# Adding the weights onto their negated high part by a transfer, in ten chunks of a down projection

## The chip, the cores and the metric

The kernel runs on one core of one Trainium2 chip. The metric is the device time of one execution in microseconds (us). The engines of the core work side by side and wait for one another by semaphores: TensorE multiplies matrices, VectorE and ScalarE work element by element, GpSimd does the same and issues transfers from a queue of its own, and SyncE issues the other transfers.

## The reference

Two layers on 512 tokens of width 1024, all in float32. Layer 0 is latent attention and then a gated feed-forward block; layer 1 is a short convolution and then another such block. What matters here is the end of the feed-forward block of layer 0, the product with `w_down`:

```python
def swiglu(h, w_gate, w_up, w_down):
    return (jax.nn.silu(h @ w_gate) * (h @ w_up)) @ w_down

for i in range(DEPTH):
    ...
    h = h + swiglu(rms_norm(h, ffn_norm[i]), ffn_w_gate[i], ffn_w_up[i], ffn_w_down[i])
return rms_norm(h, final_norm)
```

`w_down` has 2816 rows (D_FF, 22 blocks of 128) and 1024 columns.

## The kernel before

**Products in three parts.** Every float32 operand is split into a high part, rounded to the format fp32r, and the rest, operand minus high part. A product is three matmuls, high by high, low by high and high by low (`product`, lines 489 to 491), summed in a PSUM bank.

**Chunks and slots.** The weights lie in memory as one stream of chunks of up to 2048 columns on 128 partitions (1 MB). Chunks go alternately to two slots, s = 0 and 1. Each slot has `raw[s]`, where the transfer lands, and `w_hi[s]` and `w_lo[s]`, the high part and the rest, both inside a buffer that the profile calls split. A chunk j of a stage lives in slot j % 2 and passes these steps:

- SyncE's `load` (issue at line 363) waits for `w_split[s]` of the chunk before in the same slot, since until then raw is still read, and fetches the next chunk.
- ScalarE's `split` (line 937) waits until raw has landed and until TensorE is done with the chunk before in the same slot (`chunk_done[s]`), copies raw to `w_hi[s]` and raises `hi_split[s]`.
- The rest, raw minus `w_hi[s]`, goes to `w_lo[s]` and raises `w_split[s]`. In this stage VectorE makes it (line 1445). In the attention stage GpSimd does (line 460).
- TensorE waits once per chunk for `w_split[s]`, multiplies, and raises `chunk_done[s]`.

**The down projection of layer 0** takes 12 chunks, here called chunks 0 to 11. Four pairs of output tiles take three chunks each: 8, 8 and 6 blocks of rows, so 2048, 2048 and 1536 columns. A chunk of 2048 columns is 48 matmuls of 512 columns, one of 1536 is 36. Chunks 2, 5, 8 and 11 are the short ones. The two slots mean that chunk j is split while chunk j - 1 is multiplied. So chunks 3, 6 and 9, which are long, are split during a short one.

**What sets the order.** Each engine has one fixed order, and nothing is scheduled at run time. ScalarE runs `residuals`, which splits chunk c + 2 in its step c, with sizes `DOWN_AHEAD` = 1536, 2048, 2048, repeated, and squares the finished sums in every third step. In steps 9 to 11 it also prepares operands of the convolution (`conv_operands`). VectorE runs `down_round`: in every third step it adds two finished tiles to the residual (lines 1716 and 1718), makes operands for the next stage (lines 1453 and 1456) and adds squares (line 1471), and in every step it makes the rest of chunk c + 2. Steps 10 and 11 already split the first two chunks of the next stage. GpSimd's last work is the rest of a chunk in the attention stage.

Of the kernel before, what the change touches and what calls it, by code (L numbers as in the profile page):

```python
# [29 lines left out]
ALU = mybir.AluOpType  # L30
ACT = mybir.ActivationFunctionType
# [23 lines left out]
DOWN_AHEAD = (DOWN_N * 3)[2:8]  # L55
# [54 lines left out]
FIRST_PIECES = [(int(k0 >= 5), (k0 - 5 * (k0 >= 5)) * FIRST_N, (k1 - 5 * (k0 >= 5)) * FIRST_N) for k0, k1 in FIRST_K]  # L110
WARM_UP = 13
MASKED = -float(2.0 ** 93)


Q_BANKS, K_BANKS, V_BANKS, TURNED, HEAD_BANKS = (4, 5, 6), (1, 2), (4, 5), ((7, 0, 1, 3), (7, 0, 6, 0)), (3, 7)
# [60 lines left out]
def build(nc, x, head_in, positions, weights_in, out):  # L176
    with ExitStack() as ctx:
        def sb(name, cols, dt=F32):
            return ctx.enter_context(nc.sbuf_tensor(name, [P, cols], dt))

        def sem(name):
            return ctx.enter_context(nc.semaphore(name))
# [33 lines left out]
        raw = [sb(f"raw{s}", SLOT) for s in range(2)]  # L216
        split_slots = [sb(f"split{s}", 2 * SLOT + (PHASE, PLACE)[s] // 4, F32R) for s in range(2)]
        block_hi, block_lo = ([t[:, i * SLOT:(i + 1) * SLOT] for t in split_slots] for i in range(2))
        w_hi, w_lo = ([t[:, PLACE // 4 + i * SLOT:PLACE // 4 + (i + 1) * SLOT] for t in split_slots] for i in range(2))
# [16 lines left out]
        def tile(t, m, n=SEQ):  # L236
            return t[:, m * SEQ:m * SEQ + n]
# [58 lines left out]
        w_split = [sem(f"w_split{s}") for s in range(2)]  # L296
# [45 lines left out]
        part_summed, u_made = sem("part_summed"), sem("u_made")  # L342
        gate_scaled, result_added = sem("gate_scaled"), sem("result_added")
        inner_ready = sem("inner_ready")
        step = sem("step")
        own = sem("own")

# [63 lines left out]
        @block.gpsimd  # L411
        def _(pool):
            pool.wait_ge(piece_hi, 4)
            pool.dma_start(sin[:, :].bitcast(I32), positions.partition_broadcast(P)).then_inc(positions_loaded, 16)
            n = [0]

            def do(instruction):

                instruction.then_inc(own, 1)
                n[0] += 1  # L420
                pool.wait_ge(own, n[0])


            do(pool.memset(ident[:, :], 0.0))
            pool.affine_select(out=ident[:, :], in_=ident[:, :], compare_op=ALU.not_equal, fill=1.0, base=0,
                               pattern=[[-1, P]], channel_multiplier=1).then_inc(ident_made, 1)


            def add_query_squares(m):

                pool.wait_ge(squared, m + 1)
                if m > 1:
                    pool.wait_ge(query_squares_added, m - 1)
                pool.tensor_tensor(acc[:, :], acc[:, :], query_squares[m], ALU.add).then_inc(query_squares_added, 1)

            add_query_squares(1)


            key, turned_key, part = tile(work, 0), tile(work, 1), tile(work, 2)
            pool.wait_ge(trig_done, 3)  # L440
            pool.wait_ge(drained[KEY_BANK], 1)
            do(pool.tensor_tensor(turned_key, key, cos[:, :], ALU.mult))
            for to, of in SWAPPED:
                do(pool.tensor_tensor(part[to, :], key[of, :], sin[of, :], ALU.mult))
            pool.tensor_tensor(turned_key, turned_key, part, ALU.add).then_inc(key_rotated, 1)

            pool.wait_ge(key_mask, 2)
            for h in range(2):
                pool.wait_ge(key_ready, h + 1)
                rows = OTHER[h][0]  # L450
                pool.tensor_copy(tile(a_lo, KQ + KKV + h)[rows, :], mid_lo[rows, MASK_K:MASK_K + SEQ]).then_inc(key_masked, 1)
                pool.wait_ge(key_masked, h + 1)
            pool.wait_ge(rope_ready, 1)
            for m in range(2, KQ):
                add_query_squares(m)

            def split(s, n=SLOT):

                pool.wait_ge(hi_split[s], T.add(f"slot{s}") - 1)
                pool.tensor_tensor(w_lo[s][:, 0:n], raw[s][:, 0:n], w_hi[s][:, 0:n], ALU.subtract).then_inc(w_split[s], 1)  # L460


            T = Tally()
            T.add("slot0", 3)
            T.add("slot1", 3)
            split(0, UQ_N)
            T.add("rope")
            with T.loop(pool, PAIRS - 1, slot0=1, slot1=1, rope=1):
                split(1, UKV_N)
                pool.wait_ge(rope_ready, T.add("rope"))  # L470
                split(0)
            split(1)


        @block.tensor
# [453 lines left out]
        def _(act):  # L929
            T = Tally()  # L930

            def split(s, n=SLOT):

                k = T.add(f"slot{s}")
                act.wait_ge(raw_loaded[s], (k - 1) * 16)
                act.wait_ge(chunk_done[s], k - 1)
                act.activation(w_hi[s][:, 0:n], raw[s][:, 0:n], ACT.Copy).then_inc(hi_split[s], 1)  # L937
# [15 lines left out]
            def square(src, dst, ring):  # L953

                if ring:
                    wait(act, squares_added, max(0, T.add("added") - ring))
                act.activation(dst, src, ACT.Square).then_inc(squared, 1)
# [81 lines left out]
            for h in range(2):  # L1039
                act.activation(tile(a_lo, KQ + KKV + h), tile(work, 2), ACT.Copy,  # L1040
                               scale=vec[:, HEAD_MASK + h:HEAD_MASK + h + 1]).then_inc(key_ready, 1)
# [109 lines left out]
            def residuals(banks, per, sizes, norm=None, also=None):  # L1151

                chunks = KD // 2 * per
                for c in range(chunks):
                    pair, s = c // per, c % 2
                    if norm:
                        x_operands(pair, banks[pair % len(banks)], norm, lambda: split(s, sizes[0]))
                        continue
                    split(s, sizes[c % len(sizes)])
                    if c % per == per - 1:  # L1160
                        for h, b in enumerate(banks[pair % len(banks)]):
                            act.wait_ge(result_added, T.add("result"))
                            T.add(f"b{b}")
                            square(tile(xT, 2 * pair + h), tile(work, 4 + h), 2)
                    if also:
                        also(c)

            def x_operands(k, banks, norm, split_next):


                buf, half = x_form[k % 2], X_PAIR // 2

                def part_hi(n):

                    cols = slice(k * X_PAIR + n * half, k * X_PAIR + (n + 1) * half)
                    act.activation(x_hi[:, cols], buf[:, n * half:(n + 1) * half], ACT.Copy).then_inc(x_hi_made, 1)

                if k < K_PAIRS - 1:
                    split_next()
                if k > 1:  # L1180
                    act.wait_ge(x_split, T.now("x") + 2 * (k - 1))
                for h, b in enumerate(banks):
                    act.wait_ge(drained[b], T.add(f"b{b}"))
                    act.activation(tile(buf, h), tile(xT, 2 * k + h), ACT.Copy, scale=gain(norm, 2 * k + h)).then_inc(x_scaled, 1)
                act.wait_ge(x_scaled, T.add("scaled", 2))
                part_hi(0)
                for h in range(2):
                    square(tile(xT, 2 * k + h), tile(work, 4 + h), 2)
                if k == K_PAIRS - 1:
                    split_next()  # L1190
                act.wait_ge(x_formed, T.add("formed_x"))
                part_hi(1)
                if k == K_PAIRS - 1:
                    T.add("x", 2 * K_PAIRS)
# [164 lines left out]
            for c in range(0, 12, 3):  # L1359
                s = c % 2  # L1360
# [47 lines left out]
        def _(v):  # L1408
            T = Tally()
# [32 lines left out]
            def split(s, n=SLOT):  # L1442

                v.wait_ge(hi_split[s], T.add(f"slot{s}") - 1)
                v.tensor_tensor(w_lo[s][:, 0:n], raw[s][:, 0:n], w_hi[s][:, 0:n], ALU.subtract).then_inc(w_split[s], 1)  # L1445
# [214 lines left out]
            for h in range(2):  # L1660
# [4 lines left out]
                v.tensor_scalar(queries_of, own_rows, 1.0, None, ALU.mult).then_inc(query_mask, 1)  # L1665
                v.tensor_scalar(keys_of, own_rows, MASKED, None, ALU.mult).then_inc(key_mask, 1)
            key_take()
# [300 lines left out]
            def ffn(name):  # L1968
# [31 lines left out]
                def down_round(m):  # L2000
                    for c in range(6):
                        if c % 3 == 2:
                            pair = c // 3
                            banks, ms = DOWN_BANKS[pair], [m + (2 * pair + k) for k in range(2)]
                            v.wait_ge(tile_summed, T.add("summed"))
                            add_scaled(banks[0], ms[0])
                            done(c % 2)
                            add_scaled(banks[1], ms[1])
                            next_operands(ms, name)
                        split(c % 2, DOWN_AHEAD[c])  # L2010
                        if m:
                            conv_operands(c)

# [102 lines left out]
            for c in range(0, 12, 3):  # L2116
                s = c % 2
# [147 lines left out]
```

## Time and profile before

| | |
|---|---|
| median of 3 runs | 1063.09 us (1062.82 to 1064.02) |
| profiled execution, span | 1063.2 us |
| TensorE busy | 1053.6 us |
| VectorE busy | 846.8 us |
| ScalarE busy | 529.2 us |
| GpSimd busy | 41.7 us, all before 161 us |
| the 12 chunks of the down projection | about 425 to 547 us of the span |

The profiled execution's span, from the first to the last instruction, is 0.1 us over the median of the runs, so the two can be used as one. Matmuls overlap in the trace: each is shown with 0.39 us, but in this stage one starts every 0.227 us, and that distance is what counts. Chunk 2 is multiplied from 446.74 to 454.90 us, chunk 3 from there to 465.78 us.

### The profile page before, as it was taken

Reading aid. Unit: us, or ns where it says so; the run is one execution under the profiler, and the core shown is the slowest. Engines: PE = TensorE matmul, PEld = TensorE weight load, DVE = VectorE, ACT = ScalarE, POOL = GpSimd, SP = SyncE. Lnnn points to the kernel's source line nnn. Section 1 sums busy time; section 2 is a strip of 40 time slices with the busy share of each in tenths; the row PEclk is TensorE's granted clock in tenths of the full one; section 3 lists DMA queues with packets and bytes.
Section 4 is the critical chain, followed back from the end, with each engine's and each line's share of the span. In section 5 each row is a group of like instructions: output and inputs, shape, how many; then the busy total and the mean of one; then the engine's idle time right before and its main releaser. Section 6 shows DMA issues by size and latency. Waiting matters only on the chain.

```text
span 1063.2 us, 17801 instructions
## 1 busy us (share of the span) xinstructions
PE 1053.6 (99%) x6766; PEld 956.3 (90%) x6766; DVE 846.8 (80%) x1195; ACT 529.2 (50%) x755; POOL 41.7 (4%) x24
## 2 busy tenths in 40 slices
PE   9999999999999999999999999999999999999998
PEld 7888888889999999888888888888999999988997
DVE  5777775999999998734577677688999999898665
ACT  6597773745544555521343323355455545563332
POOL 0232230000000000000000000000000000000000
PEclk9999999999999999999999999999999999999999
DMA  8221112232233232233232222232332232232212
GB/s 287 100 69 46 54 70 80 80 120 108 89 118 118 82 115 108 80 109 109 78 111 91 108 97 102 80 119 80 118 118 85 113 118 99 88 109 98 92 68 80
DMA packets 16967, 106.21 MB, mean 100 GB/s; under 512 B 1888, under 2 KB 2272, under 8 KB 6432
## 3 DMA queue, kind: packets, MB, share of 16 engines
q1 hardware_dynamic: 16848, 105.43, 27.8%
q8 instruction: 25, 0.41, 0.2%
q0 software_dynamic: 80, 0.26, 0.1%
q14 instruction: 14, 0.11, 0.0%
HBM read 103.59 MB, written 2.10 MB: 99 GB/s over the span
## 4 chain that ended last, share of the span: by engine, by line
PE 94%; DVE 2%; DMA 1%; ACT 1%; issue 1%; SPq 0%; DVEq 0%
PE bank L489 30%; PE bank L491 30%; PE bank L490 30%; DMA raw<-weights_in 1%; PE bank L649 1%; ACT split L1206 1%; PE bank L635 0%; PE bank L637 0%; DVE s_lo L1804 0%; PE bank L528 0%; DVE split L1445 0%; ACT split L937 0%; DVE mid_lo L1488 0%; PE bank L891 0%; PE bank L903 0%
## 5 line engine op out<-in xcount | busy, mean ns | idle before, releaser
L489 PE MATMUL bank<-x_hi,split 128*128 128x256 f32 (+1 forms) x704 | 204.8, 291 | 0.0
L491 PE MATMUL bank<-x_hi,split 128*128 128x256 f32 (+1 forms) x704 | 204.3, 290 | 0.0
L490 PE MATMUL bank<-x_lo,split 128*128 128x256 f32 (+1 forms) x704 | 203.4, 289 | 0.0
L937 ACT ACTIVATE split<-raw 128x2048 fp32r<-128x2048 f32 (+2 forms) x51 | 90.1, 1767 | 138.6 <-PE bank L491 134.4
L1445 DVE TENSOR_TENSOR split<-raw,split 128x2048 fp32r<-128x2048 f32 (+2 forms) x43 | 92.5, 2151 | 60.1 <-ACT split L937 60.1
L489 PE MATMUL bank<-x_hi,s_hi 128*128 128x256 f32 x480 | 134.7, 281 | 0.6 <-ACT work L1216 0.6
L490 PEld LDWEIGHTS bank<-x_lo,split 128*128 128x128 f32 x704 | 132.4, 188 | 3.0 <-issue 0.5
L489 PEld LDWEIGHTS bank<-x_hi,split 128*128 128x128 f32 x704 | 132.4, 188 | 3.0 <-issue 0.5
L491 PEld LDWEIGHTS bank<-x_hi,split 128*128 128x128 f32 x704 | 132.3, 188 | 2.5
L491 PE MATMUL bank<-x_hi,s_lo 128*128 128x256 f32 x480 | 134.5, 280 | 0.0
L490 PE MATMUL bank<-x_lo,s_hi 128*128 128x256 f32 x480 | 133.8, 279 | 0.0
L489 PE MATMUL bank<-inner_hi,split 128*128 128x512 f32 (+1 forms) x342 | 127.7, 373 | 0.0
L491 PE MATMUL bank<-inner_hi,split 128*128 128x512 f32 (+1 forms) x342 | 127.6, 373 | 0.0
L490 PE MATMUL bank<-inner_lo,split 128*128 128x512 f32 (+1 forms) x342 | 127.6, 373 | 0.0
L1801 DVE TENSOR_TENSOR split<-raw,split 128x2048 fp32r<-128x2048 f32 x47 | 107.6, 2290 | 20.7 <-ACT split L1206 19.0
L1206 ACT ACTIVATE split<-raw 128x2048 fp32r<-128x2048 f32 x47 | 90.0, 1916 | 58.3 <-DVE work L1796 50.7
L489 PE MATMUL bank<-a_hi,split 128*128 128x512 f32 (+1 forms) x264 | 100.5, 381 | 1.7 <-DVE a_lo L1532 0.8
L491 PE MATMUL bank<-a_hi,split 128*128 128x512 f32 (+1 forms) x264 | 99.4, 377 | 0.0
L490 PE MATMUL bank<-a_lo,split 128*128 128x512 f32 (+1 forms) x264 | 99.4, 376 | 0.0
L1223 ACT ACTIVATE work<-bank 128x256 f32<-128x256 f32 x44 | 16.9, 384 | 164.8 <-PE bank L491 164.8
L489 PEld LDWEIGHTS bank<-x_hi,s_hi 128*128 128x128 f32 x480 | 90.3, 188 | 1.3 <-ACT work L1216 1.0
L490 PEld LDWEIGHTS bank<-x_lo,s_hi 128*128 128x128 f32 x480 | 90.3, 188 | 0.0
(276 smaller groups left out, 2206.6 us busy)
## 6 DMA issues: line engine op xcount, KB each, us to landing
raw<-weights_in SPq DMA_DIRECT2D x82, 1024.0 KB, 4.8
raw<-weights_in SPq DMA_DIRECT2D x12, 768.0 KB, 4.2
work<-x SPq DMA_DIRECT2D x4, 512.0 KB, 9.9
raw<-weights_in SPq DMA_DIRECT2D x4, 512.0 KB, 3.8
out<-head SPq DMA_DIRECT2D x3, 512.0 KB, 2.7
head<-head_in SPq DMA_DIRECT2D x1, 768.0 KB, 8.8
raw<-weights_in SPq DMA_DIRECT2D x3, 192.0 KB, 4.0
raw<-weights_in SPq DMA_DIRECT2D x1, 576.0 KB, 7.4
```

What stands on the lines that cost most here:

```text
L489: pe.matmul(o, lhs[0], rhs[0], start=start, stop=False, skip_group_check=True)
L490: pe.matmul(o, lhs[0], rhs[1], start=False, stop=False, skip_group_check=True)
L491: return pe.matmul(o, lhs[1], rhs[0], start=False, stop=stop, skip_group_check=True)
L649: tr = pe.transpose(bank[b][:, j * P:(j + 1) * P], work[:, p0:p0 + P], ident[:, :])
L937: act.activation(w_hi[s][:, 0:n], raw[s][:, 0:n], ACT.Copy).then_inc(hi_split[s], 1)
L1206: act.activation(block_hi[s][:, :], raw[s][:, :], ACT.Copy).then_inc(hi_split[s], 1)
L1223: act.activation(copies[g][0], bank[b][:, 0:HT], ACT.Copy).then_inc(drained[b], 1)
L1445: v.tensor_tensor(w_lo[s][:, 0:n], raw[s][:, 0:n], w_hi[s][:, 0:n], ALU.subtract).then_inc(w_split[s], 1)
L1801: v.tensor_tensor(block_lo[s][:, :], raw[s][:, :], block_hi[s][:, :], ALU.subtract).then_inc(w_split[s], 1)
```

## The change

For the first 10 steps of `residuals`, that is for chunks 2 to 11 of the down projection, the rest is no longer made by VectorE. ScalarE copies raw a second time, with scale -1, into `w_lo[s]`, whose format fp32r rounds it as it does the high part, so `w_lo[s]` holds minus the high part. It raises `negated[s]`. GpSimd waits for that and issues a transfer from `raw[s]` to `w_lo[s]` with `accum_op=ALU.add`, both in the on-chip memory (SBUF). It waits until the transfer has landed (`rest_added[s]`) and raises `w_split[s]` by an instruction without work. VectorE counts the slot on and does nothing for it.

```diff
+RESTS_BY_DMA = 10
...
+            def add_rest(c):
+
+                s, k, n = c % 2, c // 2 + 1, DOWN_AHEAD[c % 6]
+                pool.wait_ge(negated[s], k)
+                pool.dma_start(w_lo[s][:, 0:n], raw[s][:, 0:n], accum_op=ALU.add).then_inc(rest_added[s], 16)
+                pool.wait_ge(rest_added[s], 16 * k)
+                pool.nop().then_inc(w_split[s], 1)
+
+            for c in range(RESTS_BY_DMA):
+                add_rest(c)
...
-                    split(s, sizes[c % len(sizes)])
+                    n = sizes[c % len(sizes)]
+                    split(s, n)
+                    if c < RESTS_BY_DMA:
+                        act.activation(w_lo[s][:, 0:n], raw[s][:, 0:n], ACT.Copy, scale=-1.0).then_inc(negated[s], 1)
...
-                        split(c % 2, DOWN_AHEAD[c])
+                        if m // 4 * 6 + c < RESTS_BY_DMA:
+                            T.add(f"slot{c % 2}")
+                        else:
+                            split(c % 2, DOWN_AHEAD[c])
```

GpSimd, from the last rest of the attention stage to its end. Lines 460 (before) and 462 (now) are the subtraction, 480 is the transfer. Before:

```order
L460 TENSOR_TENSOR split1<-raw1,split1 128x2048 [waits hi_split1]
L177 UNCONDITIONAL_BRANCH
```

Now:

```order
L462 TENSOR_TENSOR split1<-raw1,split1 128x2048 [waits hi_split1]
L480 DMA split0<-raw0 128x1536 [waits negated0]
L480 DMA split1<-raw1 128x2048 [waits rest_added0,negated1]
L480 DMA split0<-raw0 128x2048 [waits rest_added1,negated0]
L480 DMA split1<-raw1 128x1536 [waits rest_added0,negated1]
L480 DMA split0<-raw0 128x2048 [waits rest_added1,negated0]
```

Each transfer has a wait for the one before it, so that never more than one is on its way.

ScalarE at the splits of chunks 2 to 5. Lines 937 (before) and 950 (now) are the high part, 957 and 970 the squares, 1175 the negated copy. Before:

```order
L937 ACTIVATE split0<-raw0 128x1536 [waits chunk_done0,raw_loaded0]
L937 ACTIVATE split1<-raw1 128x2048 [waits chunk_done1,raw_loaded1]
L937 ACTIVATE split0<-raw0 128x2048 [waits chunk_done0,raw_loaded0]
L957 ACTIVATE work<-head 128x512 [waits squares_added,result_added] x2
L937 ACTIVATE split1<-raw1 128x1536 [waits chunk_done1,raw_loaded1]
```

Now:

```order
L950 ACTIVATE split0<-raw0 128x1536 [waits chunk_done0,raw_loaded0]
L1175 ACTIVATE split0<-raw0 128x1536
L950 ACTIVATE split1<-raw1 128x2048 [waits chunk_done1,raw_loaded1]
L1175 ACTIVATE split1<-raw1 128x2048
L950 ACTIVATE split0<-raw0 128x2048 [waits chunk_done0,raw_loaded0]
L1175 ACTIVATE split0<-raw0 128x2048
L970 ACTIVATE work<-head 128x512 [waits squares_added,result_added] x2
```

The negated copy stands right behind each split and ahead of the squares.

## Rows read from the trace of the kernel before

**Rows 1.** The page, part 1: busy time by engine, share, instructions.

```profile
PE 1053.6 (99%) x6766; PEld 956.3 (90%) x6766; DVE 846.8 (80%) x1195; ACT 529.2 (50%) x755; POOL 41.7 (4%) x24
```

**Rows 2.** TensorE's waits over the whole span: total us, times, longest.

```profile
PE bank L549 <- DVE ones L1517: 1.1, 1, 1.1
PE bank L489 <- DVE split L1445: 0.9, 2, 0.7
PE bank L489 <- DVE a_lo L1532: 0.8, 1, 0.8
PE bank L489 <- ACT work L1216: 0.6, 2, 0.3
PE bank L489 <- ACT work L1069: 0.5, 1, 0.5
...
```

**Rows 3.** Windows: us, busy us of each engine, granted clock, DMA share, GB/s.

```profile
430.00:560.00 130.00, 130.00 (x573) 107.32 (x572) 73.38 (x91) 44.67 (x48) 0.00 (x0) 1.00 0.28 99
```

**Rows 4.** Timeline of ScalarE: start us, us, line, out<-in, [idle before <- releaser].

```profile
447.00 1.92 ACT L937 ACTIVATE split<-raw 128x2048 fp32r<-128x2048 f32 x1 [9.38 <-PE bank L491]
455.16 1.92 ACT L937 ACTIVATE split<-raw 128x2048 fp32r<-128x2048 f32 x1 [6.24 <-PE bank L491]
456.99 1.13 ACT L957 ACTIVATE work<-head 128x512 f32<-128x512 f32 x2
466.04 1.49 ACT L937 ACTIVATE split<-raw 128x1536 fp32r<-128x1536 f32 x1 [7.92 <-PE bank L491]
476.92 1.92 ACT L937 ACTIVATE split<-raw 128x2048 fp32r<-128x2048 f32 x1 [9.39 <-PE bank L491]
...
506.84 1.92 ACT L937 ACTIVATE split<-raw 128x2048 fp32r<-128x2048 f32 x1 [9.39 <-PE bank L491]
```

**Rows 5.** Timeline of TensorE at the end of chunk 2 and start of chunk 3.

```profile
454.68 0.39 PE L491 MATMUL bank<-inner_hi,split 128*128 128x512 f32 x1
454.90 0.39 PE L489 MATMUL bank<-inner_hi,split 128*128 128x512 f32 x1
```

**Rows 6.** Timeline of VectorE while chunk 2 is multiplied.

```profile
448.96 2.29 DVE L1445 TENSOR_TENSOR split<-raw,split 128x2048 fp32r<-128x2048 f32 x1 [7.04 <-ACT split L937]
451.17 0.68 DVE L1716 TENSOR_TENSOR work<-bank,rstd 128x512 f32<-128x512 f32 x1
451.88 0.69 DVE L1718 TENSOR_TENSOR head<-work,head 128x512 f32<-128x512 f32 x1
```

**Rows 7.** Transfers of 0 to 1063 us: count, KB each, median us from issue to landing.

```profile
raw<-weights_in SPq DMA_DIRECT2D x82, 1024.0 KB, 4.8
raw<-weights_in SPq DMA_DIRECT2D x12, 768.0 KB, 4.2
...
sin<-positions POOLq DMA_DIRECT2D x1, 256.0 KB, 8.1
```

**Rows 8.** The page, part 3: the queue's packets, MB, share of 16 engines' span.

```profile
q1 hardware_dynamic: 16848, 105.43, 27.8%
```

**Rows 9.** GpSimd's only transfer, and two windows after its issue (columns as in rows 3).

```profile
10.35 0.70 POOL L414 DMA_DIRECT2D sin<-positions  x1 [9.89 <-ACT split L975]
...
10.00:12.00 2.00, 2.00 (x11) 1.65 (x10) 1.73 (x3) 1.50 (x4) 1.41 (x3) 1.00 1.04 434
...
16.00:18.00 2.00, 2.00 (x10) 1.67 (x9) 0.61 (x1) 0.00 (x0) 0.00 (x0) 1.00 0.97 381
```

**Rows 10.** Each load of line 363 takes this long on SyncE's queue to issue.

```profile
L363 SPq DMA_DIRECT2D raw<-weights_in x13: 332/333/337, 434.4 to 552.5; - x13
```

**Rows 11.** ScalarE at chunk 11 (line 937) and the convolution's operands (1135, 1141).

```profile
525.88 1.50 ACT L937 ACTIVATE split<-raw 128x1536 fp32r<-128x1536 f32 x1 [7.91 <-PE bank L491]
527.28 2.55 ACT L1135 ACTIVATE conv_form<-head 128x512 f32<-128x512 f32 x4
530.79 1.06 ACT L1141 ACTIVATE tail_hi<-conv_form 128x1024 fp32r<-128x1024 f32 x1 [0.96 <-DVE conv_form L1753]
532.38 1.06 ACT L1141 ACTIVATE tail_hi<-conv_form 128x1024 fp32r<-128x1024 f32 x1 [0.53 <-DVE conv_form L1753]
536.76 1.92 ACT L937 ACTIVATE split<-raw 128x2048 fp32r<-128x2048 f32 x1 [3.32 <-PE bank L491]
```

More of the change, by code:

```diff
@@ L344, in build @@
         inner_ready = sem("inner_ready")
+        negated, rest_added = [sem(f"negated{s}") for s in range(2)], [sem(f"rest_added{s}") for s in range(2)]
         step = sem("step")
```

## The prediction

> **What bounds the kernel now.** I read the busy times first: TensorE is busy 1053.6 of 1063.2 us, VectorE 846.8 [rows 1]. Then TensorE's waits: over the whole span they come to 4.4 us (the five rows shown and two of 0.3 and 0.2), the longest 1.1 us, at the start [rows 2]. Then the window of 430 to 560 us, which holds the edited chunks: TensorE is busy all 130 us at a granted clock of 1.00, while VectorE has 73 us of work, ScalarE 45 and GpSimd none [rows 3]. So TensorE bounds this stretch alone, and VectorE's subtraction is off the path: the work taken away from it can bring nothing here. What is left to ask is whether the new way to a chunk's rest still ends before TensorE wants it.
>
> **How much time a chunk's rest has.** Chunk j is split while chunk j - 1 is multiplied. The tight places are chunks 3, 6 and 9: 2048 columns to split, while TensorE has only the 36 matmuls of a short chunk. For chunk 3, ScalarE starts the split at 447.00 us [rows 4], and TensorE issues chunk 3's first matmul at 454.90 us, 0.22 us behind chunk 2's last [rows 5]. The room is 454.90 - 447.00 = 7.90 us. Before, the rest is made at 448.96 + 2.29 = 451.25 us [rows 6], 3.65 us early. For the chunks that are split during a long one the starts of two splits lie 10.88 us apart (455.16 and 466.04, rows 4); less the same 8.16 - 7.90 = 0.26 us that is 10.62 us of room. The tight place comes three times, at 447.00, 476.92 and 506.84 us [rows 4].
>
> **ScalarE's part.** It gains ten copies. Two copies of 2048 columns follow each other as the split at 455.16 and the next instruction at 456.99 do, so the second starts 1.83 us behind the first and takes 1.92 us [rows 4]: the negated part is ready 3.75 us after the split's start. For 1536 columns it is 1.4 + 1.5 = 2.9 us [rows 4, 11]. Neither copy delays ScalarE's other work by anything that counts: behind a split it stands idle for 6 to 9 us [rows 4]. Queued behind it are the squares at 456.99, then 1.9 us later, with VectorE's sums behind them and ScalarE idle afterwards until 466.04. At chunk 11 the convolution's operands stand behind it: they move from 527.28 to about 528.7, and the last of this batch ends near 534.9 in place of 533.44 us, still before the next split at 536.76 [rows 11]. I take all of that at nothing; without that cover it would be 1.4 us once.
>
> **The transfer.** No row of before shows an adding transfer, nor one inside the on-chip memory, so it is bounded. From below: a plain load of the same 1024 KB takes 4.8 us from issue to landing [rows 7]. It could also be below that, since the nearest row starts in the chip's outer memory; I keep 3.85 us, where nothing would be lost, as a case. The middle: an add has to read two operands. What the loads occupy is 0.278 x 16 x 1063.2 = 4729 us of engine time for 105.43 MB [rows 8], 44.9 us per MB, over 16 engines 2.94 us for 1024 KB (1.049 MB). A second read of that size gives 4.8 + 2.94 = 7.7 us. The issue on GpSimd takes 0.70 us [rows 9] and on SyncE's queue 0.33 us [rows 10]: plus 0.4. That is 8.1 us. From above: GpSimd's only transfer took 8.1 us for 256 KB [rows 7], with the engines between 0.97 and 1.04 busy with other loads in two windows of its time [rows 9]. For the other three quarters with both reads it would be 8.1 + 0.75 x 5.9 = 12.5 us. I take 8.1: the engines are 0.28 busy here [rows 3], so that the loads of rows 7 are nearer than a transfer in the rush of the start. For 1536 columns it is 8.1 less a quarter of 5.9, 6.6 us.
>
> On the second read the Trainium skill has a rule ("Collectives: The Full Stack", section "The bandwidth ceiling: the fold count and why AG ≠ RS ≠ AR"): a reducing transfer reads two sources on one ring and so runs at about half the rate of a copy. No row of before shows it. With one read alone the middle would be 4.8 + 0.4 = 5.2 us and the loss about 4 us in place of the sum below.
>
> **Handing over.** ScalarE to GpSimd, the landing to GpSimd, and GpSimd's empty instruction to TensorE. VectorE starts 0.04 us after the split's end [rows 4, 6]; that is one handing over. I take 0.3 us for all, an estimate of several times that row, as an instruction more stands between.
>
> **The sum.** For a tight chunk 3.75 + 0.3 + 8.1 = 12.15 us after the split's start, against 7.90 us of room: TensorE stands for 4.25 us. For a short chunk 2.9 + 0.3 + 6.6 = 9.8 us, against 10.62: nothing. For chunks 4, 7 and 10 it is 12.15 again, against 10.62, but TensorE's start of the chunk before was itself 4.25 us late while ScalarE's split was not: room 14.9 us, nothing. The three stalls give 3 x 4.25 = 12.8 us. GpSimd waits in its own order, one transfer at a time, but has nothing else queued. SyncE's loads wait for `w_split` and move back with it: a load issued at about 446 us would land at about 451 us, just as the next transfer starts. They meet only where there is room (the load behind a late chunk against the transfer of the next one). VectorE loses ten subtractions, by columns 2.29 x (6 + 4 x 0.75) = 20.6 us of busy time [rows 6], at no gain. So 1063.2 + 12.8 = 1076.0 us, and as the span stands 0.1 us over the median, 1075.9: forecast 1076 us. Each us more or less of the transfer is 3 us.
>
> **Rivals.**
>
> - *As quick as a plain load or quicker.* At 3.85 us nothing is lost, at 4.8 us 3 x (4.05 + 4.8 - 7.90) = 2.9 us, 1066 us. For it: both ends lie on the chip. Against: two reads, and the slower queue. By the Trainium skill ("DMA: Bandwidth & Descriptors", section "Anatomy of one DMA — SWDGE (gpsimd) path") a transfer from this queue costs 2.0 us and its bytes at 436 GB/s, so 4.4 us by estimate, a time near 1065; but the page's fit is of copies. Chance 0.15, of which 0.12 end within 0.2%.
> - *VectorE comes out ahead.* Freed of ten subtractions it could hand over tiles earlier and take away a wait of TensorE's. It needs a wait that it ends in this stretch, and there is none [rows 3]; the two of the split's line come to 0.9 us [rows 2]. 1062 us at best, if the transfers stay under 3.85 us too. Chance 0.02.
> - *A long transfer.* At 12.5 us the three stalls are 3 x 8.65 = 26.0 us. Chunks 4, 7 and 10 are then bound by one transfer behind the other: 12.5 + 0.3 against 10.88 us, 3 x 1.9 = 5.8 us. Short chunks need 2.9 + 0.3 + 9.9 = 13.1 against 10.62 us, but only at chunk 11 does that count, as a stall before a tight chunk is taken off the tight one: 2.5 us. 1097 us. For it: GpSimd's 8.1 us for a quarter of the bytes. Against: how full the engines were. From about 10.9 us on it leaves the forecast. Chance 0.25.
> - *The clock falls in the new gaps.* TensorE has never stood for more than 1.1 us, and the granted clock is 1.00 [rows 2, 3]. A gap of 4 us is new. Were a quarter of each long chunk behind a gap run at 1.2 in place of 2.4 GHz, it would cost 0.25 x 10.88 = 2.7 us, three times 8 us: 1084 us; were it the whole chunk, 33 us. No row bears on it. Chance 0.07.
> - *VectorE and GpSimd get in each other's way* while the transfer is prepared. In the tight places VectorE runs one addition from two buffers at 451.88 us for 0.69 us [rows 6], 1.1 us behind the transfer's issue at 450.8. At most 3 x 0.7 = 2.1 us more: 1078 us. The Trainium skill ("SBUF — State Buffer", section "SBUF: two separate sides") says that this queue's descriptors are written by GpSimd, which VectorE can lock out. Chance 0.05.
>
> That the change does not do what it says can be left aside: ten transfers and ten copies stand in the new order.
>
> **How the numbers follow.** Forecast 0.46, the rivals 0.15, 0.02, 0.25, 0.07 and 0.05. Half of the long transfer's cases lie above 1097, so I end the range at 1102; below, 1064.5 stands for a transfer of some 4.3 us, half a us under the plain load, and cuts off the cases in which nothing is lost. About 0.2% (2.1 us) is what a measurement of this kernel can tell from no change: faster 0.02, within it 0.12, slower 0.86.
>
> **What would show it.** TensorE should wait for GpSimd before chunks 3, 6 and 9, about 4.3 us each, and hardly before any other. ScalarE's second copy should end 3.75 us after the first one's start. The transfer of 1024 KB from GpSimd should land after about 8.1 us, that of 768 KB after 6.6, and VectorE's busy time should fall by about 21 us with no other time moved. The forecast is wrong if the transfer takes less than 5 or more than 11 us, if the clock is below 1.00 behind a gap, or if chunks 4, 7 and 10 wait as well.

## The result and the profile after

The changed kernel takes 1081.18 us (median of 4 runs, 1079.77 to 1082.12) against 1062.95 us before; the ratio is 1.016, with a 95% interval of 1.0145 to 1.0174. It is 18 us slower. The forecast was 1076 us, slower, with a range of 1064.5 to 1102. One of the ten executions of e4_plain_copy below ran at a mean granted clock of 0.851 and took 1149.9 us, and it is left out of that kernel's numbers.

The page, part 1, of the changed kernel:

```profile
span 1080.3 us, 17821 instructions
PE 1059.8 (98%) x6766; PEld 959.7 (89%) x6766; DVE 827.1 (77%) x1185; ACT 545.8 (51%) x765; POOL 50.5 (5%) x34
```

Against [rows 1] VectorE has 19.7 us less work and ScalarE 16.6 us more, as written in the change. TensorE does the same 6766 matmuls and is busy 6.2 us longer, which no wait explains: something made matmuls slower. Its waits, which answer to [rows 2]:

```profile
PE bank L502 <- POOLq L482: 6.3, 2, 3.2
PE bank L502 <- DVE a_lo L1472: 3.3, 1, 3.3
PE bank L502 <- DVE split L1461: 1.6, 2, 0.8
```

Line 482 is GpSimd's empty instruction that hands a chunk over. The second row is the same kind of wait put down to VectorE, which had long been done. The timeline of TensorE shows where the three stand, ahead of chunks 3, 6 and 9 and nowhere else in the stage (start, us, and in brackets the idle time before):

```profile
457.75 0.49 PE L502 MATMUL bank<-inner_hi,split 128*128 128x512 f32 x1 [3.09 <-POOLq L482]
...
491.26 0.76 PE L502 MATMUL bank<-inner_hi,split 128*128 128x512 f32 x1 [3.29 <-DVE a_lo L1472]
...
527.58 0.49 PE L502 MATMUL bank<-inner_hi,split 128*128 128x512 f32 x1 [3.20 <-POOLq L482]
```

The way to chunk 3, from ScalarE's two copies (lines 950 and 1175) to GpSimd's issue, from the timelines of the two engines:

```profile
446.60 1.92 ACT L950 ACTIVATE split<-raw 128x2048 fp32r<-128x2048 f32 x1 [7.96 <-PE bank L504]
448.42 1.90 ACT L1175 ACTIVATE split<-raw 128x2048 fp32r<-128x2048 f32 x1
454.75 1.91 ACT L950 ACTIVATE split<-raw 128x2048 fp32r<-128x2048 f32 x1 [4.43 <-PE bank L504]
...
450.62 0.86 POOL L480 DMA_DIRECT2D split<-raw  x1 [10.80 <-ACT split L1175]
458.76 0.86 POOL L480 DMA_DIRECT2D split<-raw  x1 [7.28 <-ACT split L1175]
```

The copies end 448.42 + 1.90 - 446.60 = 3.72 us after the split's start, GpSimd issues 0.30 us later, and the transfer lands 7.0 us after that. The issues of the whole kernel (count, KB each, median us to landing), then line 480 by itself in two windows, the first with chunk 3's transfer and the second with chunk 4's:

```profile
split<-raw POOLq DMA_DIRECT2D x6, 1024.0 KB, 7.8
split<-raw POOLq DMA_DIRECT2D x4, 768.0 KB, 5.7
...
DMA to landing us min/median/max: 7.0/7.0/7.0
...
DMA to landing us min/median/max: 8.5/8.5/8.5
```

The 7.8 us is a median of two kinds: 7.0 to 7.1 us at chunks 3, 6 and 9, 8.5 to 8.6 us at chunks 4, 7 and 10, which meet a load (one is issued at 457.8 us and lands 4.6 us later, and chunk 4's transfer is issued at 458.76). 450.62 + 7.0 = 457.62, and TensorE starts at 457.75.

The granted clock, third from the end in each row, behind the first gap, in and behind the second and behind the third (windows: us; busy us of TensorE, weight loads, VectorE, ScalarE, GpSimd; clock; DMA share; GB/s):

```profile
457.75:461.20 3.45, 3.45 (x15) 2.86 (x16) 2.12 (x4) 1.76 (x3) 0.86 (x1) 1.00 0.70 217
...
488.00:491.20 3.20, 0.00 (x0) 0.00 (x0) 3.09 (x6) 3.13 (x2) 0.00 (x0) 0.91 0.66 133
491.30:494.70 3.40, 3.40 (x8) 2.72 (x9) 1.88 (x3) 1.52 (x3) 0.86 (x1) 0.50 0.79 234
494.70:498.00 3.30, 3.30 (x10) 2.52 (x10) 0.00 (x0) 0.00 (x0) 0.00 (x0) 0.58 1.01 218
...
527.60:531.00 3.40, 3.40 (x9) 2.73 (x10) 1.99 (x3) 1.63 (x3) 0.86 (x1) 0.58 0.69 231
```

At 0.50 TensorE runs at 1.2 GHz in place of 2.4: the second and third matmul behind the second gap start 0.43 us apart (491.82 and 492.25 us), where 0.227 is usual. It is the second part of the loss. Behind the first gap the clock stayed at 1.00.

**Counting by the stage.** ScalarE's split of chunk 2 and that of the first chunk after the down projection stand for the same two points of the work in every kernel. Before they lie at 436.12 and 536.76 us, 100.64 us apart; now at 435.77 and 551.33, 115.56 us. The stage has lost 14.92 us. From ScalarE's split at the end of a short chunk (454.75, 488.07 and 524.47 us) to that at the end of the long chunk behind it (469.03, 505.44 and 540.45) it is 14.28, 17.37 and 15.98 us in place of 10.88: 3.40 + 6.49 + 5.10 = 14.99 us, which is all of it. Of each, the gap is 3.1 to 3.3 us, and in the first place, where the clock stayed, 0.3 us more is lost at its edges. Of that, 0.16 us is the way of counting: a matmul is shown with 0.39 us but the next starts 0.227 us behind it, so the idle time shown begins 0.16 us late. Another 0.1 us is real, since the second matmul behind the gap follows the first after 0.32 us in place of 0.227. The rest, about 2.9 and 1.6 us in the second and third place and nothing in the first, is the clock.

Outside the stage the changed kernel's profiled execution takes 964.7 us and the kernel before's 962.6 us. That belongs to no part of the change; it is taken up below.

### The profile page after: what moved, and what is told of

It is laid out like the page before. It is cut to its first block, busy times and chain, and to the rows that moved or that the text cites. A ratio compares the mean times of both kernels' runs of the same rounds, so it can differ in the third digit from the quotient of the medians.

```text
span 1080.3 us, 17821 instructions
## 1 busy us (share of the span) xinstructions
PE 1059.8 (98%) x6766; PEld 959.7 (89%) x6766; DVE 827.1 (77%) x1185; ACT 545.8 (51%) x765; POOL 50.5 (5%) x34
## 4 chain that ended last, share of the span: by engine, by line
PE 89%; issue 4%; DVE 2%; DMA 2%; ACT 2%; POOL 1%; SPq 0%; DVEq 0%; POOLq 0%; ACTq 0%
PE bank L502 29%; PE bank L504 29%; PE bank L503 29%; DMA split<-raw 1%; PE bank L662 1%; ACT split L1222 1%; DMA raw<-weights_in 1%; PE bank L650 0%; PE bank L648 0%; ACT split L950 0%; ACT split L1175 0%; DVE s_lo L1820 0%; POOL work L446 0%; PE bank L541 0%; POOL acc L436 0%
## 5 line engine op out<-in xcount | busy, mean ns | idle before, releaser
L502 PE MATMUL bank<-inner_hi,split 128*128 128x512 f32 (+1 forms) x342 | 129.9, 380 | 9.6 <-POOLq L482 6.3
L504 PE MATMUL bank<-inner_hi,split 128*128 128x512 f32 (+1 forms) x342 | 129.3, 378 | 0.0
L1817 DVE TENSOR_TENSOR split<-raw,split 128x2048 fp32r<-128x2048 f32 x47 | 107.6, 2290 | 20.7 <-ACT split L1222 19.7
L504 PEld LDWEIGHTS bank<-x_hi,s_lo 128*128 128x128 f32 x480 | 90.2, 188 | 0.0
```

What stands on the lines that cost most here:

```text
L502: pe.matmul(o, lhs[0], rhs[0], start=start, stop=False, skip_group_check=True)
L504: return pe.matmul(o, lhs[1], rhs[0], start=False, stop=stop, skip_group_check=True)
L1817: v.tensor_tensor(block_lo[s][:, :], raw[s][:, :], block_hi[s][:, :], ALU.subtract).then_inc(w_split[s], 1)
```

## Experiments

Theory A: the loss is made at chunks 3, 6 and 9 alone. The way over ScalarE and the transfer is longer than the short chunk that should cover it, and the clock falls behind some of the gaps. Theory B: a good part comes from the transfers' traffic or from ScalarE's second copies wherever they are. In the table the median is that of the kernel, with the median of the kernel before in the same round in brackets, "stage" is the distance of the two splits named above in the profiled execution, "outside" is the span less the stage.

| kernel | median, us | ratio to before (95%) | stage, us | outside, us |
|---|---|---|---|---|
| before | | | 100.64 | 962.6 |
| changed | 1081.18 (1062.95) | 1.016 (1.0145 to 1.0174) | 115.56 | 964.7 |
| e1_loose | 1067.36 (1064.15) | 1.0030 (1.0018 to 1.0042) | 103.06 | 962.6 |
| e2_tight | 1080.30 (1064.15) | 1.0151 (1.0127 to 1.0175) | 116.72 | 961.6 |
| e3_vector_adds | 1064.43 (1064.15) | 1.0004 (0.9992 to 1.0016) | 100.58 | 962.0 |
| e4_plain_copy | 1065.52 (1064.15) | 1.0013 (1.0000 to 1.0027) | 102.72 | 961.9 |
| e5_negated_first | 1070.16 (1063.42) | 1.0059 (1.0038 to 1.0080) | 105.52 | 961.7 |
| e6_filled | 1077.50 (1063.42) | 1.0116 (1.0086 to 1.0145) | 112.63 | 963.1 |
| e7_loose_negated_first | 1064.93 (1063.11) | 1.0015 (1.0005 to 1.0026) | 100.61 | 964.0 |
| e8_filled_all | 1073.53 (1063.11) | 1.0099 (1.0083 to 1.0116) | 110.50 | 961.4 |

**e1_loose and e2_tight: which chunks.** The ten chunks are parted. Steps 1, 4 and 7 of `residuals` are chunks 3, 6 and 9.

```diff
-RESTS_BY_DMA = 10
+RESTS_BY_DMA = (0, 2, 3, 5, 6, 8, 9)    # e1_loose
+RESTS_BY_DMA = (1, 4, 7)                # e2_tight
```

> The seven chunks that are split during a long chunk (2, 4, 5, 7, 8, 10, 11) keep the adding transfer, the tight ones (3, 6, 9) go back to VectorE. Theory A (the loss is made at the tight chunks alone, by gaps and by what the clock does behind them): no wait of TensorE for GpSimd, clock 1.00 all through, 1063 us like the kernel before. Theory B (a good part of the loss comes from the transfers' traffic or from ScalarE's extra copies, wherever they are): seven tenths of the 18 us, about 1075 us.

> Only chunks 3, 6 and 9 keep the adding transfer. Theory A: three gaps of 3.1 to 3.3 us as in the changed kernel, and the whole loss, 1079 to 1082 us. Theory B: three tenths of the loss, about 1068 us.

The three transfers of e2_tight bring the whole loss, 16.1 us in the stage, and the seven of e1_loose 2.4 us, which neither theory had expected. Where those come from, TensorE's timeline of e1_loose says:

```profile
465.51 0.50 PE L502 MATMUL bank<-inner_hi,split 128*128 128x512 f32 x1 [0.29 <-POOLq L482]
...
496.30 0.50 PE L502 MATMUL bank<-inner_hi,split 128*128 128x512 f32 x1 [0.57 <-POOLq L482]
...
527.17 0.50 PE L502 MATMUL bank<-inner_hi,split 128*128 128x512 f32 x1 [0.65 <-POOLq L482]
```

These are the starts of chunks 4, 7 and 10. Their way from the split's start to TensorE's is as long as the tight ones' (11.07, 11.08 and 11.44 us here; 11.15, 11.35 and 11.26 at chunks 3, 6 and 9 of the changed kernel), and their room is 10.6 us. In the changed kernel they have no gap, because the late start of the chunk before gave them more than 3 us. So e1_loose takes three gaps away and uncovers three others, 1.5 us of idle time and 0.3 us each at the edges. Theory A stands, with six places in place of three.

e2_tight also shows that a gap of one length can go either way. Windows over its first gap and behind it:

```profile
453.90:457.00 3.10, 0.04 (x1) 0.00 (x0) 2.92 (x5) 2.95 (x3) 0.00 (x0) 0.94 0.74 151
457.00:460.00 3.00, 2.97 (x7) 2.40 (x8) 2.97 (x5) 0.00 (x0) 0.00 (x0) 0.50 0.58 193
460.00:463.00 3.00, 3.00 (x14) 2.45 (x14) 1.29 (x1) 0.00 (x0) 0.00 (x0) 0.99 0.40 100
```

TensorE stood for 3.09 us, as at the first gap of the changed kernel, where the clock stayed.

**e3_vector_adds: which step of the way.** ScalarE makes all ten negated copies; VectorE adds raw to them where it subtracted before, and GpSimd does nothing.

```diff
-            for c in range(RESTS_BY_DMA):
-                add_rest(c)
...
+                            v.wait_ge(negated[c % 2], g // 2 + 1)
+                            lo_part, n = w_lo[c % 2], DOWN_AHEAD[c]
+                            v.tensor_tensor(lo_part[:, 0:n], raw[c % 2][:, 0:n], lo_part[:, 0:n], ALU.add).then_inc(w_split[c % 2], 1)
```

> ScalarE makes the negated copy for all ten chunks, but VectorE adds raw to it in place of the transfer. This splits the two parts of the new way. Rest ready 3.75 + 2.3 = 6.1 us after the split's start against 7.9 us of room, so if the transfer is what is too long, no gap and 1063 us. If ScalarE's second copy alone were the cause, three gaps would stay.

```profile
430.00:560.00 130.00, 130.00 (x574) 107.29 (x573) 73.60 (x89) 60.05 (x55) 0.00 (x0) 1.00 0.28 99
```

The stage is back at 100.58 us, and TensorE has no gap in it. The second copy on ScalarE costs nothing where VectorE's 2.3 us stand behind it. It is the 7.0 us of the transfer that make the way longer than the room, and only with them does the copy's 1.83 us count too (e5_negated_first).

**e4_plain_copy: what the add costs.** The transfer copies raw over the negated part and adds nothing, so the rest of every such chunk is wrong, and the output with it. The waits and the work of the other engines stay.

```diff
-                pool.dma_start(w_lo[s][:, 0:n], raw[s][:, 0:n], accum_op=ALU.add).then_inc(rest_added[s], 16)
+                pool.dma_start(w_lo[s][:, 0:n], raw[s][:, 0:n]).then_inc(rest_added[s], 16)
```

> The transfer copies raw over the negated part and adds nothing, so the low part is wrong and the output with it; all waits stay. If the second read of the add costs time as the prediction's sum had it, the transfer of 1024 KB takes 5.0 to 5.5 us in place of 7.0 at a tight chunk, the gaps shrink to about 1.3 us and the clock stays at 1.00: 1067 us. If an add costs no more than a copy, it stays near 7 us and 1081 us.

```profile
split<-raw POOLq DMA_DIRECT2D x6, 1024.0 KB, 4.2
split<-raw POOLq DMA_DIRECT2D x4, 768.0 KB, 3.5
...
454.05 0.49 PE L502 MATMUL bank<-inner_hi,split 128*128 128x512 f32 x1 [0.38 <-POOLq L482]
```

A copy inside the on-chip memory lands after 4.2 us, below the 4.8 us of a load from outside [rows 7]. The add costs 7.0 - 4.2 = 2.8 us more, for 1024 KB without a load beside it. The gaps are 0.4 to 0.5 us, less than expected, since the copy is quicker than expected, and the stage is 2.1 us over the kernel before's.

**e5_negated_first: taking 1.83 us off the way.** ScalarE makes the negated copy ahead of the high part. GpSimd waits for the high part too before it hands the chunk over, by when that has long been made.

```diff
+                pool.wait_ge(hi_split[s], 19 + k)
...
-                    split(s, n)
-                    if c < RESTS_BY_DMA:
+                    if c in RESTS_BY_DMA and per == 3:
+                        k = T.add(f"slot{s}")
+                        act.wait_ge(raw_loaded[s], (k - 1) * 16)
+                        act.wait_ge(chunk_done[s], k - 1)
                         act.activation(w_lo[s][:, 0:n], raw[s][:, 0:n], ACT.Copy, scale=-1.0).then_inc(negated[s], 1)
+                        act.activation(w_hi[s][:, 0:n], raw[s][:, 0:n], ACT.Copy).then_inc(hi_split[s], 1)
```

> ScalarE makes the negated copy first and the high part second, so the transfer starts 1.83 us earlier in each chunk. If a gap is the chain copy, copy, transfer less the room, each of the three shrinks from about 3.2 to 1.4 us, the clock doesn't fall behind so short a gap, and the time is 1063 + 3 x 1.4 = 1067 us. If the transfer is held back by something else (a load, a lock), the gaps stay.

```profile
PE bank L503 <- POOLq L483: 4.0, 3, 1.5
...
454.70 0.49 PE L503 MATMUL bank<-inner_hi,split 128*128 128x512 f32 x1 [1.26 <-POOLq L483]
...
454.70:457.70 3.00, 3.00 (x13) 2.49 (x14) 2.49 (x5) 3.00 (x4) 0.86 (x1) 1.00 0.58 190
```

Each gap is 1.8 to 1.9 us shorter, and the clock behind all three is 1.00. The stage loses 4.9 us: 4.0 of gaps and 0.3 at the edges of each. The whole kernel came out at 1070.2 us where 1067 was expected. It is 6.3 us over its kernel before by the ratio, 1.4 us more than the stage shows; what these are is open. In this order of the two copies a third of the loss is left, for no other work.

**e6_filled and e8_filled_all: what makes the clock fall.** The changed kernel, with matmuls that nothing uses in the gaps. The function of the diff runs for c = 0 to 5 twice, so that c == 3 stands for chunks 3 and 9. e8_filled_all writes the two rounds out and fills at chunks 3, 6 and 9.

```diff
+                    if c == 3:                      # e6_filled; in e8_filled_all: if fill:
+                        taken(0)
+                        for _ in range(14):
+                            pe.matmul(bank[0][:, 0:P], ones[:, :], ident[:, :], start=True, stop=True)
```

> The changed kernel, with 14 matmuls of 128 columns into an unused bank (about 0.19 us each, 2.6 us) ahead of TensorE's wait for chunks 3 and 9, not of chunk 6. Nothing uses what they make. If the clock falls because TensorE stands still, the granted clock stays at 1.00 behind the gap of chunk 9 and still falls, in some executions, behind that of chunk 6: 1081 less 2 us, about 1079. If it falls for another reason (the transfers, the time in the kernel), it falls at chunk 9 as before and the time stays at 1081 us.

> The changed kernel with 14 matmuls of 128 columns into an unused bank ahead of TensorE's wait for chunks 3, 6 and 9 alike (the loop over the two halves of the stage is written out for that; nothing uses what these matmuls make). If standing still makes the clock fall, it stays at 1.00 in all three places, each long chunk behind a filled gap costs 3.4 us more than in the kernel before, and the time is 1063.5 + 10.3 = 1074 us. If the written-out loop or the transfers cost something of their own, it stays above 1076 us.

Windows of e6_filled: the filled gap at chunk 3, the open one at chunk 6 and what follows it, and behind the filled one at chunk 9:

```profile
453.00:456.50 3.50, 3.50 (x30) 3.35 (x29) 3.21 (x6) 3.26 (x2) 0.00 (x0) 1.00 0.74 150
...
486.40:489.70 3.30, 0.06 (x1) 0.00 (x0) 3.10 (x6) 3.15 (x2) 0.00 (x0) 1.00 0.70 142
489.70:493.00 3.30, 3.25 (x8) 2.63 (x9) 1.97 (x3) 1.61 (x3) 0.86 (x1) 0.51 0.76 236
...
524.80:528.00 3.20, 3.20 (x14) 2.62 (x15) 1.97 (x3) 1.61 (x3) 0.86 (x1) 1.00 0.65 215
```

The three long chunks take 14.27, 16.06 and 14.32 us here: 3.4, 5.2 and 3.4 us more than 10.88. With all three filled they take 14.17, 14.21 and 14.17 us in e8_filled_all, a loss of 3.3 us each, the stage's loss is 9.9 us, and the window of the whole stage is without an idle moment at a clock of 1.00:

```profile
430.00:560.00 130.00, 130.00 (x616) 109.05 (x615) 45.05 (x68) 54.19 (x50) 8.63 (x10) 1.00 0.61 164
```

The transfers and the work of the other engines are the changed kernel's. So it is TensorE's standing still that lets the clock fall, and the difference of the two stages, 115.56 - 110.50 = 5.1 us, is what it cost in the profiled execution of the changed kernel. Over all executions the two kernels lie further apart, 7.7 us by the medians and 6.5 by the ratios, each of which is good to about 1.6 us. The forecasts of 1079 and 1074 us stood against 1077.5 and 1073.5 us. The one execution of e6_filled whose mean clock was 1.000 took 1073.7 us.

**e7_loose_negated_first: the small gaps of e1_loose.** Its seven transfers with the order of e5.

> Seven transfers as in e1_loose (not at chunks 3, 6 and 9), and ScalarE makes the negated copy ahead of the high part there, so that each transfer starts 1.83 us earlier. In e1_loose chunks 4, 7 and 10 came 0.3 to 0.65 us late. Theory A (the 3 us of e1_loose are these three small gaps): no wait for GpSimd is left, and the time is that of the kernel before, 1063 to 1064 us. Theory B (the transfers' traffic or ScalarE's copies cost something wherever they are): the 3 us stay, 1067 us.

```profile
430.00:560.00 130.00, 130.00 (x573) 107.28 (x572) 60.11 (x83) 55.57 (x54) 6.04 (x7) 1.00 0.51 148
```

TensorE is busy all 130 us and does in them as many matmuls, 573, as in [rows 3], with the DMA share at 0.51 in place of 0.28: the traffic of seven transfers slows no matmul. The stage is at 100.61 us. Yet the ratio is 1.0015, 1.6 us, with an interval that leaves 1 out, and by theory A 1063 to 1064 us were expected against 1064.9. What these 1.6 us are is open. The profiled execution has nothing of them in the stage, but its outside part is 964.0 us.

**The outside part.** It goes from 961.4 to 964.7 us over the ten kernels, which are the same there. One source is visible: in both feed-forward loops a round (from one of ScalarE's copies at line 1223 or 1239 to that two further on) takes either 19.60 or 19.79 us throughout, that is 1% more or less for each matmul. The kernel before was profiled with 19.79 in layer 0 and 19.60 in layer 1, the changed one the other way round, so these two come out even, and 1.4 of the 2.1 us by which they differ outside arise before the first of these loops (its first copy is at 236.47 and 237.83 us). What chooses the pace wasn't tried. It makes single executions differ by up to 2 us a loop; the kernel before ranges from 1062.1 to 1068.4 us over its runs.

No version that beats the kernel before was in sight, since TensorE is busy there all through the stage; the best of them only hide the transfers again.

## Why the prediction was right

The places, the mechanism and the way of each gap were forecast, and the transfer was taken too long. One thing came that the sum had left out, the clock. The prediction named a clock below 1.00 behind a gap as a sign that it is wrong, and behind two of the three gaps the clock was 0.50 and 0.58. The total came out near all the same, for the reason given under the clock.

- **The bound.** TensorE bound the stage, and VectorE's 19.7 us less (forecast 20.6) brought nothing. Shown by e7_loose_negated_first, where VectorE has 13 us less to do between 430 and 560 us and the stage takes what it took.
- **The places.** Gaps were forecast at chunks 3, 6 and 9 and nowhere else; so it was. That chunks 4, 7 and 10 would be covered by the late start of the chunk before was right too, and e1_loose shows the cover gone.
- **ScalarE's part.** 3.75 us forecast, 3.72 measured. Its other work moved without effect.
- **Handing over.** 0.3 us forecast; 0.30 us up to GpSimd's issue and 0.13 us from the landing to TensorE, 0.43 together.
- **The transfer.** This term was mis-sized: 8.1 us forecast, 7.0 measured. The part put down for the second read was right in size, 2.94 against the 2.8 us that the add costs (e4_plain_copy). What was too long is what it was added to: 4.8 us of a load from outside plus 0.4 for GpSimd's queue, where a copy within the on-chip memory from that queue takes 4.2 us. The rule on two reads, which the Trainium skill ("Collectives: The Full Stack", section "The bandwidth ceiling: the fold count and why AG ≠ RS ≠ AR") states for the reducing step of a collective, is borne out here in its direction: the add takes 7.0 / 4.2 = 1.67 times the copy, with the fixed part in both. The Trainium skill's fit for a transfer of this queue ("DMA: Bandwidth & Descriptors", section "Anatomy of one DMA — SWDGE (gpsimd) path") gives 4.4 us by estimate, and the copy took 4.2 us here.
- **Meeting the loads.** Forecast only where there is room; measured 8.5 to 8.6 in place of 7.0 us at chunks 4, 7 and 10, at no cost. In e1_loose, where no load stands beside them, the same three take 6.9, 7.0 and 7.3 us.
- **VectorE against GpSimd.** A rival with a chance of 0.05. VectorE's addition at line 1732 starts with GpSimd's issue at all three tight chunks (450.62, 483.93 and 520.34 us). In e5_negated_first it starts 1.8 us behind the issue of chunk 3 (449.39 and 447.59). The issue takes 0.86 us both times and the transfer lands after 7.0 and 6.9 us, so nothing of such a lock is seen.
- **The sum.** Three late starts of 4.25 us, 12.8 us, were forecast. Counted as in the sum, from 0.227 us behind the last matmul of the short chunk to the first of the long one, they are 3.25, 3.45 and 3.36, together 10.1 us (the gaps shown, 3.09 + 3.29 + 3.20 = 9.6 us, begin 0.16 us later each). The sum did not have the 0.1 us or so that the first matmul takes longer.
- **The clock.** Given as a rival with a chance of 0.07 and priced at 8 us, since no row bore on it. It came, beside the gaps and not in place of them, and smaller: 4.5 us by the long chunks' times, 5.1 us by e8_filled_all. This is the term that the sum put at nothing. The forecast of 12.8 us against 14.9 us in the stage is near because gaps too long by 2.7 us in all and a clock left out, 4.5 us, nearly make up for each other. That part of the agreement is luck.
- **A slip in a rival.** The long transfer's short chunk was taken at 9.9 us. By the prediction's own rule it is 12.5 less a quarter of 5.9, 11.0 us, which makes that rival 1099 in place of 1097 us. With 7.0 us measured it plays no part.
- **Against the median.** The forecast took the span of 1063.2 us as 0.1 us over the median time. In all runs since, time is 1.7 to 2.0 us above span, so that by estimate the execution profiled before was one of about 1065 us, 1.9 us over the median. As the sum was only a difference, it did no harm. Of the 5 us by which 1081.2 is over 1076, 2.1 are the stage's in the profiled execution. Where the other 3 are is open, since only one execution was profiled. Part of it may be the clock: the mean granted clock of the others was 0.993, 0.993 and 0.992 against 0.994, and each 0.001 less stands for 2.2 of the 1080 us at the lower clock, by estimate 1.1 us lost. The differences between executions outside the stage are of the same size. In e2_tight, with 16.1 us in the stage, the ratio gives 16 us.

## What to carry to other kernels

A step that is off the path is free only up to the shortest piece of work that covers it: look for the short chunk in a sequence of unequal ones, and compare the whole way from start to hand-over with that, not with the mean. Here a transfer of 7 us in place of 2.3 us on an engine made a way of 11.1 us, which stood out by 0.3 to 0.65 us even behind a chunk of 10.9 us (e1_loose). With the copy that the transfer needs made first, it was hidden behind 10.9 us (e7_loose_negated_first) and still not behind 8.2 (e5_negated_first). When TensorE's wait grows from nothing to 3 us, count the clock behind it as well: in this kernel it cost half as much again as the gaps.

## What was not expected of the hardware

- An add by transfer of 1024 KB within the on-chip memory takes 7.0 us and one of 768 KB 5.7 us from GpSimd's issue to landing, a copy 4.2 and 3.5 us. GpSimd's issue takes 0.86 us for the add and 0.53 us for the copy. Beside a load the add of 1024 KB takes 8.4 to 9.0 us (changed kernel and e5_negated_first).
- A gap of 3.09 us let the clock fall in e2_tight and not in the changed kernel. Of the seven open gaps of 3.06 to 3.61 us in these two kernels and e6_filled the clock fell at six, for 3 to 6 us, and at none of the three of 1.3 to 1.5 us in e5_negated_first. In three of the six it fell before TensorE had started again (0.91, 0.94 and 0.79 in the windows over the gaps), in the others with the restart or after it.
- The same loop runs at one of two paces, 19.60 or 19.79 us a round, in executions of the same code and at a granted clock of 1.00.
